# Squares of the residual stream gathered behind the eight updates and splits at seven norms of a decoder trunk

## The chip, the cores and the metric

One core of one Trainium2 chip runs the whole program. The metric is device microseconds of that core for one execution. Three runs of the kernel before gave 2433.85, 2435.99 and 2439.0 us; their median is 2435.99 us. Engines are named as in the profile: PE is TensorE (PEld its weight loads), DVE is VectorE, ACT is ScalarE, POOL is GpSimd, SP is the engine that issues the weight transfers.

## The reference, cut to what matters

The reference is a two-layer decoder trunk over 512 tokens of width 1024, in float32. Each layer adds four results to the residual stream h: a SwiGLU feed-forward (FFN, inner width 2816), a mixer, a cross-attention into 256 memory tokens, and a second FFN. Ahead of each stands an RMS norm of h, and one more stands at the very end:

```
def rmsnorm(x, g):
    y = xf * lax.rsqrt(jnp.mean(xf * xf, axis=-1, keepdims=True) + EPS)
    return y * g
...
    h = h + 0.5 * swiglu(rmsnorm(h, ffn1_norm[layer]), ...)
    hn = rmsnorm(h, mix_norm[layer])
    h = h + mix
    h = h + cross_attn(rmsnorm(h, xa_norm[layer]), mem_n, ...)
    h = h + 0.5 * swiglu(rmsnorm(h, ffn2_norm[layer]), ...)
```

The nine norms are numbered 0 to 8 in the kernel. Norm 0 works on the input, norms 1, 4 and 5 follow an FFN and lead into another projection, norms 2, 3, 6 and 7 follow an output projection (of a mixer or a cross-attention), and norm 8 is the final one.

## The kernel before, in words

**Layout.** Everything lies feature by token: h is eight chunks (k = 0 to 7) of 128 partitions by 512 tokens. A projection multiplies by weights first and is scaled by the norm's factor rstd afterwards, when its result is read from PSUM, so that PE need not wait for rstd. What PE must have is x, the gained h, split into an upper part (rounded, written by ACT in L849) and a lower part (the rest, written by DVE in L1276, `lower(k)`). Each product is three matmuls of 128x512: L310 (upper weight, upper x), L311 (upper, lower) and L312 (lower, upper).

**Weights.** A stream of 381 blocks of 128x1024 comes by DMA into two slots. POOL splits each half block in the same way: a tiny gate operation (L279), which waits until PE has left the slot, then the upper part (L280) and the lower part (L284). It takes halves in the order a, a, b, b over a pair of blocks. It takes an a half when the a half of the block two earlier has been used, and a b half when that block is done (`block_done`).

**A norm between stages.** For each chunk k, DVE waits for the finished PSUM bank and adds it to h (L1301, `h_ready`); ACT waits for that and writes the upper part of x (L849), then the square of h into one of two buffers `sq` (L871). DVE writes the lower part of chunk k-1 (L1276), then adds the square of chunk k-1 to the sum in `tg` (L1283 copies the first one, L1286 adds the other seven, `add_square`). The square k may only be written when the sum has taken in square k-2 (`sq_added`). So DVE's order is: update k, lower k-1, add k-1, update k+1, and so on.

**PE at a norm.** `project` (L340) runs the first two tiles of the next stage side by side, chunk by chunk. It waits before each chunk for the lower part of x (`x_lo`); 48 matmuls in all, six to a chunk. From chunk 4 on it also wants the b halves of both weight blocks (`split_ready`). Directly after these comes `mean_square` (L320): it waits until all eight squares are in the sum, and multiplies by a matrix of ones (L324). Only then do tiles three and four follow. ACT takes the square root (L877), DVE the reciprocal rstd (L1309), and the results of the stage are read with it (L1399, L1325).

After an FFN, PE finishes the eight PSUM banks in quick succession (six matmuls apart) and DVE follows it. After an output projection the banks come one by one, 24 matmuls apart, so that only the last chunk's update, lower part and square are left when the last tile ends.

Of the kernel before, what the change touches and what calls it, by code (L numbers as in the profile page):

```python
# [32 lines left out]
ACT = mybir.ActivationFunctionType  # L33
# [5 lines left out]
KC = D // P  # L39
# [124 lines left out]
def build_trunk(nc, xT, memT, pos, vecs, w_alpha, s5b, s5c, mats, mask, rows, stream, out):  # L164
    with ExitStack() as ctx:
        def sb(name, shape, dt=F32):
            return ctx.enter_context(nc.sbuf_tensor(name, shape, dt))
# [3 lines left out]
        def S(name):  # L171
            if name not in sems:
                sems[name] = ctx.enter_context(nc.semaphore(name))
            return sems[name]

        ps = ctx.enter_context(nc.psum_tensor("ps", [P, 8, T], F32))
        h = sb("h", [P, KC, T])
# [8 lines left out]
        sq = sb("sq", [P, 2, T])  # L186
# [37 lines left out]
        def gain(n, k):  # L224
            return vec[:, V_GAIN + 8 * n + k:V_GAIN + 8 * n + k + 1]
# [620 lines left out]
        def _(act):  # L846
            def hi(dst, src, count, **kw):

                act.activation(dst, src, ACT.Copy, **kw).then_inc(S("x_hi"), 1)  # L849

            def norm(n):

                to = NORM_TO[n] if n < 8 else None
                for k in range(KC):
                    if n == 0:
                        if k == 0:
                            act.wait_ge(S("vec_in"), 16)
                            act.wait_ge(S("x_in0"), 16)
                        if k == 2:
                            act.wait_ge(S("x_in1"), 16)  # L860
                    else:
                        act.wait_ge(S("h_ready"), 8 * (n - 1) + k + 1)
                    if to is not None:
                        if n in (1, 4, 5) and k >= 4:
                            f = {1: 0, 4: 1, 5: 2}[n]

                            act.wait_ge(S("block_done"), FFN_AT[f] + FFN_BLOCKS - (2 if k < 6 else 0))
                        hi(X[to][:, k, 0, :], h[:, k, :], 0, scale=gain(n, k))
                    if 8 * n + k >= 2:
                        act.wait_ge(S("sq_added"), 8 * n + k - 1)  # L870
                    act.activation(sq[:, k % 2, :], h[:, k, :], ACT.Square).then_inc(S("sq_ready"), 1)  # L871
                if n == 0:
                    act.wait_ge(S("eps_set"), 2)
                act.wait_ge(S("ssq_done"), n + 1)
                if n >= 1:
                    act.wait_ge(S("rstd_ready"), n)
                act.activation(std[:], ps[:, SSQ_BANK, :], ACT.Sqrt, bias=epsc[:, 0:1]  # L877
                               ).then_inc(S("std_ready"), 1)
# [336 lines left out]
            def fill(l, banks, n):  # L1215
                for _ in range(n):
                    if kv_next[0] < 16:
                        kv_out(l, kv_next[0], banks)
                        kv_next[0] += 1

            norm(0)
            ffn(0, lambda: memory_split(0), s5_begin)
            norm(1)
            s5(lambda j: fill(0, KV_BANKS, j - 13) if j >= 14 else None)
            fill(0, KV_BANKS, 2)
# [3 lines left out]
            fill(0, KV_BANKS, 16)  # L1229
            glu_split()  # L1230
            norm(2)
            cross(0)
            norm(3)
# [20 lines left out]
        def _(dve):  # L1254
# [13 lines left out]
            def norm(n, factor, mm_sem, mm_base, banks):  # L1268

                to = NORM_TO[n] if n < 8 else None  # L1270

                def lower(k):
                    if to is None:
                        return
                    dve.wait_ge(S("x_hi"), X_LO_NORM[n] + k + 1)
                    dve.scalar_tensor_tensor(X[to][:, k, 1, :], h[:, k, :], gain(n, k),  # L1276
                                             X[to][:, k, 0, :].bitcast(F32), ALU.mult, ALU.subtract
                                             ).then_inc(S("x_lo"), 1)

                def add_square(k):  # L1280
                    dve.wait_ge(S("sq_ready"), 8 * n + k + 1)
                    if k == 0:
                        ins = dve.tensor_copy(tg[:, 0, :], sq[:, 0, :])  # L1283
                    else:
                        dve.wait_ge(S("sq_added"), 8 * n + k)
                        ins = dve.tensor_tensor(tg[:, 0, :], tg[:, 0, :], sq[:, k % 2, :], ALU.add)  # L1286
                    ins.then_inc(S("sq_added"), 1)

                if n == 0:
                    for k in range(KC):  # L1290
                        lower(k)
                        add_square(k)
                else:
                    for k in range(KC):
                        if mm_sem is not None and k < 7:
                            dve.wait_ge(mm_sem, mm_base[0] + k + 1)
                        elif mm_sem is not None:
                            dve.wait_ge(S("block_done"), mm_base[1])
                        else:
                            dve.wait_ge(S("block_done"), mm_base[0] + k + 1)  # L1300
                        dve.scalar_tensor_tensor(h[:, k, :], ps[:, banks[k], :], factor, h[:, k, :],  # L1301
                                                 ALU.mult, ALU.add).then_inc(S("h_ready"), 1)
                        if k >= 1:
                            lower(k - 1)
                            add_square(k - 1)
                    lower(KC - 1)
                    add_square(KC - 1)
                dve.wait_ge(S("std_ready"), n + 1)
                dve.reciprocal(rstd[:], std[:]).then_inc(S("rstd_ready"), 1)  # L1309
                dve.wait_ge(S("rstd_ready"), n + 1)  # L1310

            def norm_after_ffn(n, f):
                norm(n, 0.5, S("down_out"), (7 * f, FFN_AT[f] + FFN_BLOCKS), DOWN_BANKS)

            def norm_after_out(n, o):
                norm(n, 1.0, None, (OUT_AT[o],), [BANKS[t % 4] for t in range(8)])
# [525 lines left out]
            dve.memset(epsc[:, 0:1], EPS).then_inc(S("eps_set"), 1)  # L1842
            dve.memset(epsc[:, 1:2], float(np.pi / 2)).then_inc(S("eps_set"), 1)
            norm(0, 1.0, None, (0,), None)
            ffn(0, lambda: memory_split(0), s5_output_matrices)
            norm_after_ffn(1, 0)
# [167 lines left out]
```

## Time and profile before

| | |
|---|---|
| median of three runs | 2435.99 us (2433.85 to 2439.0) |
| profiled execution, span from first to last instruction | 2432.6 us |
| PE busy | 2301.4 us, 95% |
| POOL busy | 1738.1 us, 71% |
| DVE busy | 1154.7 us, 47% |
| ACT busy | 435.1 us, 18% |
| mean granted TensorE clock | 0.973 |

The profiled execution has no time of its own beside its span; the three runs were executed apart from it. The median stands 3.4 us above the span. Busy time is a share of the whole span; a stretch of 20 us at a norm can be bound by another engine than the span is. In the timelines a duration is from issue to end, so that it holds the time in which an instruction stands issued and has not got what it needs.

### The profile page before, as it was taken

What the parts mean: (1) busy time and instruction counts of PE and PEld (TensorE: products, weight loads), DVE (VectorE), ACT (ScalarE), POOL (GpSimd) and SP (SyncE); (2) the same over time, 40 slices, a digit from 0 to 9 for tenths busy, and PEclk for the clock granted to TensorE, in tenths of its full rate; (3) what the DMA queues carried; (4) which work ended last, traced back from release to release, by engine and by line L of the source; (5) the groups of instructions that cost most, each with busy time, mean ns of one, the idle gap of its engine ahead of it and who ended that gap; (6) DMA issues with size and microseconds to landing.
All of it is one profiled execution on the core that took longest, in us unless ns stands there. A gap on an engine that the chain in (4) does not pass through costs nothing.

```text
span 2432.6 us, 31471 instructions
## 1 busy us (share of the span) xinstructions
PE 2301.4 (95%) x10068; PEld 1820.2 (75%) x10068; DVE 1154.7 (47%) x1468; ACT 435.1 (18%) x752; POOL 1738.1 (71%) x2287
## 2 busy tenths in 40 slices
PE   7999999888789999999999999999987999999997
PEld 6888786445678688888778888877765777888886
DVE  7577717998644342224244223144598333322314
ACT  2122212002221221111122101120134222111011
POOL 7788877565648377878787788876764746777874
PEclk9999999897889999999999999999999999999998
DMA  4244334222212123333232323332221212323332
GB/s 158 90 144 146 126 95 134 78 91 78 70 57 95 49 83 95 98 96 100 91 108 87 99 95 95 100 94 83 78 74 53 81 58 77 96 95 97 96 96 82
DMA packets 117312, 226.02 MB, mean 93 GB/s; under 512 B 13040, under 2 KB 13312, under 8 KB 116864
## 3 DMA queue, kind: packets, MB, share of 16 engines
q1 hardware_dynamic: 110736, 203.61, 26.5%
q10 hardware_dynamic: 6512, 21.52, 2.6%
q8 instruction: 45, 0.74, 0.1%
q14 instruction: 19, 0.16, 0.0%
HBM read 214.59 MB, written 10.49 MB: 93 GB/s over the span
## 4 chain that ended last, share of the span: by engine, by line
PE 79%; DVE 15%; issue 2%; ACT 2%; POOL 1%; DMA 0%; SPq 0%; ACTq 0%; DVEq 0%; POOLq 0%
PE ps L310 24%; PE ps L311 24%; PE ps L312 24%; DVE tg L1286 1%; DVE arena L1738 1%; PE ps L728 1%; DVE col L1737 1%; PE ps L753 1%; DVE x L1276 1%; DVE sg L1652 1%; PE ps L602 1%; DVE sg L1650 1%; PE ps L643 1%; PE ps L613 1%; DVE arena L1757 0%
## 5 line engine op out<-in xcount | busy, mean ns | idle before, releaser
L310 PE MATMUL ps<-x,w_split 128*128 128x512 f32 (+1 forms) x2872 | 1126.3, 392 | 39.6 <-POOL w_split L284 17.4
L311 PE MATMUL ps<-x,w_split 128*128 128x512 f32 (+1 forms) x2872 | 1110.3, 387 | 0.0
L312 PE MATMUL ps<-x,w_split 128*128 128x512 f32 (+1 forms) x2872 | 1110.0, 386 | 0.0
L284 POOL TENSOR_TENSOR w_split<-w_raw,w_split 128x512 fp32r<-128x512 f32 x762 | 1021.5, 1341 | 63.5
L279 POOL TENSOR_TENSOR gate<-gate 128x1 f32<-128x1 f32 x758 | 257.7, 340 | 602.2 <-PE ps L312 601.9
L310 PEld LDWEIGHTS ps<-x,w_split 128*128 128x128 f32 x2872 | 544.4, 190 | 180.6 <-POOL w_split L284 28.0
L311 PEld LDWEIGHTS ps<-x,w_split 128*128 128x128 f32 x2872 | 544.5, 190 | 110.1 <-issue 4.8
L312 PEld LDWEIGHTS ps<-x,w_split 128*128 128x128 f32 x2872 | 543.9, 189 | 108.8
L280 POOL TENSOR_SCALAR w_split<-w_raw 128x512 fp32r<-128x512 f32 x762 | 509.4, 669 | 4.5 <-DMA w_raw<-in_stream 4.5
L1371 DVE TENSOR_TENSOR x<-arena,x 128x512 fp32r<-128x512 f32 x88 | 87.3, 1008 | 284.6 <-ACT x L941 284.6
L1328 DVE TENSOR_TENSOR tu<-ps,rstd 128x512 f32<-128x512 f32 x88 | 60.7, 689 | 319.5 <-PE ps L312 319.5
L887 ACT ACTIVATE sg<-tg 128x512 f32<-128x512 f32 x88 | 55.6, 632 | 652.1 <-DVE tg L1325 646.9
L1325 DVE TENSOR_TENSOR tg<-ps,rstd 128x512 f32<-128x512 f32 x88 | 60.6, 689 | 192.1 <-PE ps L312 191.3
L1334 DVE TENSOR_TENSOR arena<-sg,tu 128x512 f32 (+1 forms) x88 | 107.6, 1222 | 27.3 <-ACT sg L887 17.8
L1301 DVE SCALAR_TENSOR_TENSOR h<-ps,h 128x512 f32<-128x512 f32 x64 | 44.0, 688 | 142.9 <-PE ps L312 142.4
L941 ACT ACTIVATE x<-arena 128x512 fp32r (+1 forms) x88 | 53.7, 628 | 313.1 <-PE ps L312 312.4
L849 ACT ACTIVATE x<-h,vec 128x512 fp32r<-128x512 f32 x64 | 46.2, 722 | 210.7 <-DVE h L1301 206.9
L1399 DVE TENSOR_TENSOR arena<-ps,rstd 128x512 f32<-128x512 f32 x45 | 30.7, 689 | 101.4 <-PE ps L312 100.9
L1276 DVE SCALAR_TENSOR_TENSOR x<-h,vec,x 128x512 fp32r<-128x512 f32 x64 | 67.9, 1060 | 7.9 <-ACT x L849 7.9
L1286 DVE TENSOR_TENSOR tg<-tg,sq 128x512 f32<-128x512 f32 x63 | 70.0, 1110 | 0.1
L310 PE MATMUL ps<-w_split,x 128*128 128x256 f32 (+1 forms) x192 | 66.4, 346 | 1.3 <-POOL w_split L284 1.2
L311 PE MATMUL ps<-w_split,x 128*128 128x256 f32 (+1 forms) x192 | 61.1, 318 | 0.0
(234 smaller groups left out, 1576.5 us busy)
## 6 DMA issues: line engine op xcount, KB each, us to landing
w_raw<-in_stream SPq DMA_DIRECT2D x762, 256.0 KB, 2.6
s_tables<-kv ACTq DMA_DIRECT2D x16, 512.0 KB, 3.4
arena<-s_tables ACTq DMA_DIRECT2D x16, 512.0 KB, 3.3
out<-h ACTq DMA_DIRECT2D x8, 256.0 KB, 2.2
h<-in_xT SPq DMA_DIRECT2D x1, 1536.0 KB, 8.7
arena<-in_memT SPq DMA_DIRECT2D x1, 1024.0 KB, 10.5
arena<-in_memT ACTq DMA_DIRECT2D x1, 1024.0 KB, 4.8
h<-in_xT SPq DMA_DIRECT2D x1, 512.0 KB, 3.9
```

The lines of the kernel that those rows point to most:

```text
L279: pool.tensor_tensor(gate[:, 0:1], gate[:, 1:2], gate[:, 1:2], ALU.add)
L280: pool.tensor_scalar(W[:, s, 0, c], raw[:, s, c], 1.0, 0.0, ALU.mult, ALU.add).then_inc(S(f"w_hi{'ab'[half]}"), 1)
L284: pool.tensor_tensor(W[:, s, 1, c], raw[:, s, c], W[:, s, 0, c].bitcast(F32), ALU.subtract).then_inc(split_ready if half else S("half_spli ...
L310: pe.matmul(dst, wh, xh, start=start, stop=False)
L311: pe.matmul(dst, wh, xl, start=False, stop=False)
L312: return pe.matmul(dst, wl, xh, start=False, stop=stop)
L1276: dve.scalar_tensor_tensor(X[to][:, k, 1, :], h[:, k, :], gain(n, k), X[to][:, k, 0, :].bitcast(F32), ALU.mult, ALU.subtract).then_inc(S(" ...
L1286: ins = dve.tensor_tensor(tg[:, 0, :], tg[:, 0, :], sq[:, k % 2, :], ALU.add)
L1325: dve.tensor_tensor(tg[:, s, :], ps[:, BANKS[2 * s], :], rstd[:], ALU.mult).then_inc(S("gate_ready"), 1)
L1328: dve.tensor_tensor(tu[:, s, :], ps[:, BANKS[2 * s + 1], :], rstd[:], ALU.mult).then_inc(S("up_ready"), 1)
L1334: dve.tensor_tensor(dst, sg[:, s:s + 1, :], tu[:, s:s + 1, :], ALU.mult).then_inc(S("hid_done"), 1)
L1371: dve.tensor_tensor(X[xo][:, ch:ch + 1, 1, :], hid[:, d, :], X[xo][:, ch:ch + 1, 0, :].bitcast(F32), ALU.subtract).then_inc(S("x_lo"), 1)
```

## The change

At norms 1 to 7, ACT first writes all eight upper parts and then all eight squares; DVE first does all eight updates and lower parts and then the copy and the seven additions. Norms 0 and 8 keep their order. The number of instructions, their operands and the two `sq` buffers stay as they are, and so does the order on PE, POOL and SP.

```diff
+            def square(n, k):
+                if 8 * n + k >= 2:
+                    act.wait_ge(S("sq_added"), 8 * n + k - 1)
+                act.activation(sq[:, k % 2, :], h[:, k, :], ACT.Square).then_inc(S("sq_ready"), 1)
...
                         hi(X[to][:, k, 0, :], h[:, k, :], 0, scale=gain(n, k))
-                    if 8 * n + k >= 2:
-                        act.wait_ge(S("sq_added"), 8 * n + k - 1)
-                    act.activation(sq[:, k % 2, :], h[:, k, :], ACT.Square).then_inc(S("sq_ready"), 1)
+                    if n in (0, 8):
+                        square(n, k)
+                if n not in (0, 8):
+                    for k in range(KC):
+                        square(n, k)
...
                         if k >= 1:
                             lower(k - 1)
-                            add_square(k - 1)
+                            if n == 8:
+                                add_square(k - 1)
                     lower(KC - 1)
-                    add_square(KC - 1)
+                    for k in range(KC - 1 if n == 8 else 0, KC):
+                        add_square(k)
```

## Rows read from the trace of the kernel before

**Rows 1.** The page, its first part: busy us, share, instructions of each engine

```profile
PE 2301.4 (95%) x10068; PEld 1820.2 (75%) x10068; DVE 1154.7 (47%) x1468; ACT 435.1 (18%) x752; POOL 1738.1 (71%) x2287
```

**Rows 2.** Waits of PE over the span: us in total, times, longest

```profile
PE ps L310 <- DVE x L1276: 6.9, 10, 1.3
```

**Rows 3.** Timeline of PE at norm 1: start us, us, line, [idle before <-releaser]

```profile
387.45 0.39 PE L310 MATMUL ps<-x,w_split 128*128 128x512 f32 x1
...
397.77 0.50 PE L310 MATMUL ps<-x,w_split 128*128 128x512 f32 x1 [1.31 <-DVE x L1276]
...
401.61 1.02 PE L324 MATMUL ps<-tg,ones 128*128 128x512 f32 x2
```

**Rows 4.** Timeline of DVE at norm 1: begin, a cycle, last addition

```profile
378.13 0.69 DVE L1301 SCALAR_TENSOR_TENSOR h<-ps,h 128x512 f32<-128x512 f32 x1 [1.46 <-PE ps L312]
...
380.09 1.23 DVE L1276 SCALAR_TENSOR_TENSOR x<-h,vec,x 128x512 fp32r<-128x512 f32 x1
...
388.10 0.74 DVE L1276 SCALAR_TENSOR_TENSOR x<-h,vec,x 128x512 fp32r<-128x512 f32 x1
388.76 1.77 DVE L1286 TENSOR_TENSOR tg<-tg,sq 128x512 f32<-128x512 f32 x1
390.45 0.68 DVE L1301 SCALAR_TENSOR_TENSOR h<-ps,h 128x512 f32<-128x512 f32 x1
...
399.99 0.68 DVE L1286 TENSOR_TENSOR tg<-tg,sq 128x512 f32<-128x512 f32 x1
```

**Rows 5.** Timeline of PE at norm 2: first matmul of the pair, mean square

```profile
771.71 0.39 PE L310 MATMUL ps<-x,w_split 128*128 128x512 f32 x1
...
782.59 0.59 PE L324 MATMUL ps<-tg,ones 128*128 128x512 f32 x1
```

**Rows 6.** Timeline of DVE at norm 2, last two lower parts

```profile
772.51 1.52 DVE L1276 SCALAR_TENSOR_TENSOR x<-h,vec,x 128x512 fp32r<-128x512 f32 x1
...
774.56 1.10 DVE L1276 SCALAR_TENSOR_TENSOR x<-h,vec,x 128x512 fp32r<-128x512 f32 x1
```

**Rows 7.** Timeline of POOL at norm 2

```profile
774.05 1.06 POOL L280 TENSOR_SCALAR w_split<-w_raw 128x512 fp32r<-128x512 f32 x1
775.20 1.60 POOL L284 TENSOR_TENSOR w_split<-w_raw,w_split 128x512 fp32r<-128x512 f32 x1
...
782.21 0.19 POOL L279 TENSOR_TENSOR gate<-gate 128x1 f32<-128x1 f32 x1 [0.75 <-PE ps L312]
```

**Rows 8.** Timeline of DVE, then of POOL, at norm 0

```profile
20.25 1.77 DVE L1286 TENSOR_TENSOR tg<-tg,sq 128x512 f32<-128x512 f32 x1
21.95 0.74 DVE L1276 SCALAR_TENSOR_TENSOR x<-h,vec,x 128x512 fp32r<-128x512 f32 x1
22.61 1.09 DVE L1286 TENSOR_TENSOR tg<-tg,sq 128x512 f32<-128x512 f32 x1
...
22.04 1.12 POOL L280 TENSOR_SCALAR w_split<-w_raw 128x512 fp32r<-128x512 f32 x1
```

**Rows 9.** Lines of DVE over the span: duration ns min/median/max, first, last start

```profile
L1283 DVE COPY tg<-sq x9: 412/416/839, 7.9 to 2408.6; 128x512 f32<-128x512 f32 x9
...
L1301 DVE SCALAR_TENSOR_TENSOR h<-ps,h x64: 677/692/692, 378.1 to 2416.2; 128x512 f32<-128x512 f32 x64
```

**Rows 10.** Timeline of ACT and DVE at norm 8: last square, additions six, seven

```profile
2416.91 0.63 ACT L871 ACTIVATE sq<-h 128x512 f32<-128x512 f32 x1 [0.73 <-DVE h L1301]
...
2416.79 1.48 DVE L1286 TENSOR_TENSOR tg<-tg,sq 128x512 f32<-128x512 f32 x2
```

**Rows 11.** Timeline of PE after two waits

```profile
1161.24 0.50 PE L310 MATMUL ps<-x,w_split 128*128 128x512 f32 x1 [2.45 <-DVE x L1371]
...
2418.37 2.01 PE L324 MATMUL ps<-tg,ones 128*128 128x512 f32 x2 [2.22 <-issue]
```

**Rows 12.** Two windows: us, PE, PEld, DVE, ACT, POOL busy, PEclk, DMA share, GB/s

```profile
730.00:732.00 2.00, 2.00 (x6) 1.54 (x6) 0.59 (x1) 0.00 (x0) 1.88 (x3) 0.50 0.04 8
...
2418.00:2421.00 3.00, 2.01 (x2) 0.47 (x2) 0.27 (x1) 1.42 (x2) 0.00 (x0) 0.57 0.00 0
```

## The prediction

> **What bounds the kernel now.** I read the page first, then PE's waits over the span, then the timelines of PE, DVE and POOL at the seven norms that the change touches. PE is busy for 95% of the span [rows 1], so only what starts or stops PE counts. Of its waits, ten of 6.9 us together are for the lower part of x at a norm [rows 2]; nine of them, three to a norm (0.15, 1.3 and 0.7 us), lie at norms 1, 4 and 5. At none of the seven norms does PE wait for the sum of squares.
>
> *Norms 1, 4, 5 (behind an FFN).* PE's pair of tiles starts at 387.45 and has 48 matmuls. One takes (782.59 - 771.71) / 48 = 0.2267 us undisturbed [rows 5], so the pair would end at 398.33; the mean square starts at 401.61 [rows 3]. 3.28 us are lost, for DVE is slower than PE: its cycle is update, lower part, addition, and lower part plus addition alone run from 388.10 to the next update at 390.45 [rows 4]; with the 0.60 us by which an update is issued ahead of its lower part that is 2.95 us a chunk, where six matmuls take 1.36. Norms 4 and 5 show the same to 0.02 us.
>
> *Norms 2, 3, 6, 7 (behind an output projection).* The pair starts at 771.71, and the mean square follows at 782.59 without a gap [rows 5]. The last addition ends at 777.35, 5.2 us before PE asks for the sum. So here nothing is lost. The other three repeat this to 0.1 us.
>
> **Why an addition takes 0.68 or 1.77 us.** DVE and POOL keep each other out. An addition takes 0.68 us alone the last one of [rows 4] and 1.77 us when POOL's lower part (L284) is running the one at 388.76, [rows 4]. POOL is held up in its turn: its L284 at 775.20 takes 1.60 us, behind a DVE instruction that ends at 774.56 + 1.10 = 775.66, and ends at 776.80 [rows 6, 7]. The update is never held up (677 to 692 ns in 64 cases [rows 9]); it reads PSUM and one tile of SBUF. The copy of the first square is (412 to 839 ns [rows 9]). Three numbers follow: POOL's L284 ends 1.14 us behind the DVE instruction that it waited for; its L280 ends at 775.11 [rows 7]; the DVE instruction behind POOL's ends 0.55 us later, 775.66 [rows 6].
>
> When both always have work, they take turns. At norm 0 DVE's instructions end at 22.02 (behind L284), 22.69 (free) and 23.70 (behind L280, 22.04 + 1.12 = 23.16) [rows 8]: 1.70 + 0.67 + 1.01, about 3.35 us for three DVE instructions and one split half block.
>
> The Trainium skill (SBUF — State Buffer, "Who interferes with whom") states the same as a rule: the shared port pair is an exclusive lock, and issue order decides who blocks. The trace agrees with the lock (1.77 against 0.68 us). Taken strictly, the rule says that reordering moves the blocking but doesn't remove it, which speaks against a gain.
>
> **The change, part by part.** It adds and removes no instruction. It moves eight squares on ACT and a copy and seven additions on DVE behind the eighth lower part.
>
> *Lower parts come earlier.* At norm 1 the first lower part ends at 380.09 + 1.23 = 381.3 [rows 4]. Without additions two chunks take 1.14 (POOL's L284) + 0.55 (lower part behind it) + 0.60 (update, with L280 beside it) + 0.59 (second lower part) = 2.88 us; the first such pair waits 0.4 us more, since DVE comes up to PE. The seventh lower part ends at 381.3 + 3 x 2.88 + 0.4 = 390.4, the eighth at 391.0. PE wants it at 387.45 + 7 x 1.36 = 397.0, so the 3.28 us of stall in the pair are gone, if the weights are there. PE wants the second b half before chunk 4, at 392.89; POOL ends it at 392.9, the L284 behind the copy in the next paragraph. This term is worth nothing by itself, for the mean square comes next.
>
> *The sum comes later.* ACT's squares have two buffers. Square k waits for addition k-2. At norm 8 a square starts 0.04 us behind its release, takes 0.63 us, and the last addition starts at 2416.79 + 1.48 - 0.68 = 2417.59, 0.05 us behind the square's end [rows 10]; so two additions can't be faster than 0.68 + 0.04 + 0.63 + 0.05 = 1.40, 0.70 each. The ring just keeps pace and adds 0.1 us or less to some.
>  - Norm 1: lower part ends 391.0; POOL's L280 to 391.5; copy to 391.8; POOL's L284 to 392.9; first addition 393.5; then two groups of three at 3.31 us: 396.8 and 400.1. The mean square starts at 400.1 instead of 401.61: 1.5 us gained.
>  - Norm 2: the seventh lower part ends at 774.03 [rows 6], the eighth, with no addition before it, at 774.70; L280 to 775.17; copy 775.45; L284 776.59; first addition 777.14; then 780.45 and 783.76. PE asks at 782.59 and starts at 783.8: 1.2 us lost.
>
> *What it costs PE to stand.* A matmul behind a wait takes 0.50 us instead of 0.39 [rows 3], about 0.1 us at each of seven norms: 0.7 us.
>
> *What is queued behind.* On ACT the square root stands behind the eighth square; its table load (1.28 us) fits between the last square and the mean square. On DVE the reciprocal is behind the additions, and rstd is wanted only when tiles three and four are done, 10.9 us after the mean square. It takes 0.7 + 3.4 us there. Both are hidden. On SP and POOL nothing is moved; POOL's next half waits for PE's first tile of the pair (782.21 [rows 7]) in both kernels.
>
> *Sum.* 3 x -1.5 + 4 x 1.2 + 0.7 = +1.0 us. Against the span: 2432.6 + 1.0 = 2433.6. The median stood 3.4 us above the span: **2437.0 us**.
>
> *Bounds of the unknown cost.* The trace doesn't show additions back to back with POOL at work; how often POOL gets in between is the unknown. It moves all seven norms the same way. Never: copy and seven additions take 0.35 + 7 x 0.70 = 5.25 us; the sum is ready at 396.3 and 779.95, no norm waits for it, and the whole 3 x 3.28 = 9.8 us is gained. At most: POOL has three L284 to do before it must wait for PE at norm 2; with no overlap they take 1.14 + 2 x 1.95 us (L280, L284 and gate) on top of 7 x 0.70 behind the copy's end: 775.45 + 9.9 = 785.4, 1.6 us later than my value. Seven norms so: +11.5, in all +12.5. I take the value between, as it goes by the alternation at norm 0 [rows 8], the nearest row.
>
> **Rivals.**
>  1. *One L284 less in between* (faster). If POOL's last L284 comes only behind the seventh addition, or DVE passes it over, the sum is 1.14 us earlier everywhere: norm 2 loses nothing (782.6), norm 1 gains 2.6. -7.8 + 0.7 = -7.1: 2429. With POOL left out altogether it is -9.8: 2426. For it: DVE's next instruction is issued before the last one ends. Against: at norm 0 POOL did get its turns.
>  2. *DVE pauses for each square, and POOL takes each pause* (slower). The wait for a square opens a gap of some 0.1 us behind an addition; if POOL's L280 and L284 both take one, and POOL's pieces no longer share time with DVE, the sum is up to 1.6 us later at all seven. It decides once the delay passes 0.55 us a norm (0.55 x 7 = 3.9 above +1.0). Time: some 2444, at most 2448.5.
>  3. *The clock falls while PE stands at the mean square* (slower). At norm 8 PE waited 2.22 us, and its two matmuls took 2.01 instead of 1.02 us [rows 11, 3], at a granted clock of 0.57 [rows 12], near the lower level of 1.2 GHz. The mean square would lose 1.0 us, and if the half clock of the other window [rows 12] then holds for 4 us (my assumption), 2.0 us more go with it. 3 us a norm, 21 us in all: 2458. Against it: a wait of 2.45 us left the next matmul at 0.50 us [rows 11], and the waits forecast here are 1.2 to 1.5 us.
>
> **How the numbers follow.** About 0.2% (4.9 us) is what a measurement of this kernel tells from no change. Forecast (-3 to +5 us): 0.55. Rival 1: 0.17. Rival 2: 0.23. Rival 3: 0.05. Same holds the forecast's chance, less a little that spills over: 0.54. Faster: rival 1, 0.18. Slower: rivals 2 and 3, 0.28. For 8 in 10 the range takes in most of rivals 1 and 2, from 2429.0 to 2445.0; the forecast's own range is 2433 to 2441.
>
> **What would show it.** In the profile after, PE's waits at L310 for L1276 should be gone, and a wait at L324 for the sum (`tg`, L1286) should be there seven times, at 1 to 2 us. The mean square of norm 1 should stand 22.0 us behind its first update (before: 401.61 - 378.13 = 23.5), that of norm 2 11.9 us behind the last update's start (before 10.7). Additions should be 0.68, 1.0 and 1.8 us long in turn. What would make it wrong: additions all at 0.68 (rival 1), more than four of seven held up (rival 2), or a granted clock under 1.00 at these norms (rival 3).

## The result, and the profile after

The changed kernel is **slower**: 2451.44 us (median of four runs, 2448.47 to 2453.67) against 2437.38 us for the kernel before in the same comparison. The ratio is 1.0069, with a 95% interval of 1.0046 to 1.0093, so some 17 us, 11 to 23 us; the two medians differ by 14.1 us. I had forecast 2437.0 us and a range of 2429.0 to 2445.0; the measured time lies outside it, on the side of rivals 2 and 3. The profiled execution went from a span of 2432.6 to 2451.9 us; that of the changed kernel is the longest of its four (2453.67 us), 1.8 us above its own span.

PE's waits over the span (us in total, times, longest), first in the kernel after. Before, there was no wait at the mean square (L324) at these norms, and the waits for the lower part were 6.9 us in ten pieces [rows 2].

```profile
PE ps L324 <- DVE tg L1293: 19.2, 7, 3.4
...
PE ps L310 <- DVE x L1283: 2.1, 3, 1.1
```

No wait for the lower part is left at norms 1, 4 and 5, and seven waits for the sum of squares have come. (The three that the second line counts lie at norm 0.) Here are the mean squares of norms 1 to 7, from the timeline of PE (start, us, line, and in brackets the idle time before and its releaser):

```profile
403.84 2.08 PE L324 MATMUL ps<-tg,ones 128*128 128x512 f32 x2 [3.41 <-DVE tg L1293]
787.00 1.13 PE L324 MATMUL ps<-tg,ones 128*128 128x512 f32 x2 [3.06 <-DVE tg L1293]
918.11 2.08 PE L324 MATMUL ps<-tg,ones 128*128 128x512 f32 x2 [3.06 <-DVE tg L1293]
1287.40 1.13 PE L324 MATMUL ps<-tg,ones 128*128 128x512 f32 x2 [1.75 <-DVE tg L1293]
1654.87 1.13 PE L324 MATMUL ps<-tg,ones 128*128 128x512 f32 x2 [1.75 <-DVE tg L1293]
1957.55 1.13 PE L324 MATMUL ps<-tg,ones 128*128 128x512 f32 x2 [3.06 <-DVE tg L1293]
2085.39 2.07 PE L324 MATMUL ps<-tg,ones 128*128 128x512 f32 x2 [3.06 <-DVE tg L1293]
```

All seven waits are longer than the 1.2 to 1.5 us that I had in mind. And three of the seven mean squares take 2.08 us instead of 1.02 [rows 3]. The windows (us, PE, PEld, DVE, ACT, POOL busy, PEclk, DMA share, GB/s) show why, first behind norm 1, then behind norm 2, last behind norm 4:

```profile
403.00:405.00 2.00, 1.16 (x3) 0.65 (x3) 0.79 (x1) 0.00 (x0) 1.92 (x4) 0.50 0.31 49
405.00:407.00 2.00, 2.00 (x6) 1.19 (x5) 0.33 (x1) 0.69 (x1) 0.77 (x1) 0.50 0.31 100
407.00:409.00 2.00, 2.00 (x6) 1.61 (x5) 2.00 (x1) 0.00 (x0) 0.00 (x0) 0.50 0.38 121
...
788.00:790.00 2.00, 2.00 (x7) 1.57 (x6) 1.12 (x1) 1.82 (x2) 0.94 (x1) 0.58 0.23 90
...
1287.00:1289.00 2.00, 1.60 (x5) 1.02 (x6) 0.35 (x1) 0.43 (x1) 2.00 (x3) 1.00 0.31 107
```

Behind norm 1 the granted clock is 0.50, the lower of the two levels (1.2 GHz), for the whole of these 6 us; behind norm 2 it falls only once PE works again; behind norm 4, after a wait of 1.75 us, it stays at 1.00.

DVE at norm 1 of the kernel after, as the timeline gives it (L1283 is the lower part, L1290 the copy, L1293 an addition):

```profile
379.68 0.69 DVE L1308 SCALAR_TENSOR_TENSOR h<-ps,h 128x512 f32<-128x512 f32 x1 [1.46 <-PE ps L312]
...
390.89 1.84 DVE L1283 SCALAR_TENSOR_TENSOR x<-h,vec,x 128x512 fp32r<-128x512 f32 x2
392.65 0.84 DVE L1290 COPY tg<-sq 128x512 f32<-128x512 f32 x1
393.60 10.19 DVE L1293 TENSOR_TENSOR tg<-tg,sq 128x512 f32<-128x512 f32 x7
```

ACT's fourth to sixth square in the same stretch, from the timeline of ACT:

```profile
395.22 0.63 ACT L854 ACTIVATE sq<-h 128x512 f32<-128x512 f32 x1 [1.06 <-DVE tg L1293]
396.40 0.63 ACT L854 ACTIVATE sq<-h 128x512 f32<-128x512 f32 x1 [0.54 <-DVE tg L1293]
398.10 0.63 ACT L854 ACTIVATE sq<-h 128x512 f32<-128x512 f32 x1 [1.07 <-DVE tg L1293]
```

And one turn of POOL:

```profile
395.21 0.62 POOL L280 TENSOR_SCALAR w_split<-w_raw 128x512 fp32r<-128x512 f32 x1
395.91 1.61 POOL L284 TENSOR_TENSOR w_split<-w_raw,w_split 128x512 fp32r<-128x512 f32 x1
```

The eighth lower part ends at 390.89 + 1.84 = 392.73, 13.05 us behind the first update (forecast: 12.9). The seven additions then take 10.19 us. Each square is released by an addition, so the squares' starts date the additions: they end at 395.2, 396.4, 398.1, in steps of 1.2 and 1.7 us. That is 2.9 us for **two** additions and one split half block, where I had 3.31 us for three. POOL's L280 at 395.21 takes its undisturbed 0.62 us: it got the port at the moment an addition ended, and the next addition waited for it.

### The profile page after: what moved, and what is told of

Read it like the earlier page. It is cut to its first block, busy times and chain, and to the rows that moved or that the text cites. A ratio compares the mean times of both kernels' runs of the same rounds, so it can differ in the third digit from the quotient of the medians.

```text
span 2451.9 us, 31471 instructions
## 1 busy us (share of the span) xinstructions
PE 2302.1 (94%) x10068; PEld 1817.2 (74%) x10068; DVE 1173.7 (48%) x1468; ACT 439.8 (18%) x752; POOL 1742.2 (71%) x2287
## 4 chain that ended last, share of the span: by engine, by line
PE 60%; DVE 17%; POOL 10%; issue 10%; ACT 1%; DMA 0%; POOLq 0%; SPq 0%; DVEq 0%; ACTq 0%
PE ps L310 19%; PE ps L312 18%; PE ps L311 18%; POOL w_split L284 5%; POOL w_split L280 4%; DVE tg L1293 2%; POOL gate L279 2%; DVE arena L1747 1%; DVE col L1746 1%; DVE x L1283 1%; DVE sg L1659 1%; DVE sg L1661 1%; DVE h L1308 1%; DVE tu L1668 1%; PE ps L728 1%
## 5 line engine op out<-in xcount | busy, mean ns | idle before, releaser
L310 PE MATMUL ps<-x,w_split 128*128 128x512 f32 (+1 forms) x2872 | 1127.0, 392 | 34.8 <-POOL w_split L284 19.2
L284 POOL TENSOR_TENSOR w_split<-w_raw,w_split 128x512 fp32r<-128x512 f32 x762 | 1025.7, 1346 | 63.6
L280 POOL TENSOR_SCALAR w_split<-w_raw 128x512 fp32r<-128x512 f32 x762 | 505.7, 664 | 4.6 <-DMA w_raw<-in_stream 4.6
L1293 DVE TENSOR_TENSOR tg<-tg,sq 128x512 f32<-128x512 f32 x63 | 77.9, 1236 | 5.6 <-DVE tg L1293 0.5
L1283 DVE SCALAR_TENSOR_TENSOR x<-h,vec,x 128x512 fp32r<-128x512 f32 x64 | 67.3, 1057 | 8.2 <-ACT x L849 8.0
```

The lines of the kernel that those rows point to most:

```text
L280: pool.tensor_scalar(W[:, s, 0, c], raw[:, s, c], 1.0, 0.0, ALU.mult, ALU.add).then_inc(S(f"w_hi{'ab'[half]}"), 1)
L284: pool.tensor_tensor(W[:, s, 1, c], raw[:, s, c], W[:, s, 0, c].bitcast(F32), ALU.subtract).then_inc(split_ready if half else S("half_spli ...
L310: pe.matmul(dst, wh, xh, start=start, stop=False)
```

## The experiments

My theory from the trace of the changed kernel had two parts. **Turns of two:** an addition waits for the end of the addition before it (`sq_added` at 8n + k), so DVE is never queued at the port when POOL's next instruction is, and POOL gets in between any two additions. **The clock:** PE then stands at the mean square for so long that its clock falls, which costs time beyond the wait. Rivals were the two square buffers as the cause of DVE's pauses, and a loss spread alike over all norms.

### Which norms lose

```diff
-                    if n in (0, 8):
+                    if n not in (1, 4, 5):
                         square(n, k)
-                if n not in (0, 8):
+                if n in (1, 4, 5):
...
-                            if n == 8:
+                            if n not in (1, 4, 5):
                                 add_square(k - 1)
```

> New order at norms 1, 4 and 5 alone. Theory (turns of two and the clock: POOL's split and two additions take turns, and PE stands at the mean square until the clock falls): at each of these norms the stall of 3.3 us in the pair goes, a wait at the mean square comes (3.4 us at norm 1, 1.75 us at norms 4 and 5 in the changed kernel's trace), and at norm 1 some 3 us of half clock follow. 3 x -3.3 + 6.9 + 3 + 0.3 = about +0.4 us against the kernel before, so within 3 us of it. Rival (my forecast's stepping, 1.5 us gained at each): -4.5 us.

Measured: 2436.29 us against 2436.07, ratio 0.9999 (0.9986 to 1.0013): level with the kernel before, as expected. PE's waits at its mean squares are 6.8 us in three pieces. The table under "What the norms cost, from row to row" shows that the sum behind the expectation was not right in its parts: the kernel is level without any price of the clock.

The same edit with (2, 3, 6, 7) in the place of (1, 4, 5):

> New order at norms 2, 3, 6 and 7 alone. Theory (turns of two and the clock): all the loss of the changed kernel is here, 4 x (3.1 us wait + 1 to 2 us of half clock) less what the stages behind take up: +12 to +18 us, the same as the whole change within 3 us. Rival (the loss is spread over all seven norms alike): 4/7 of it, +8 us.

Measured: 2454.59 us, ratio 1.0083 (1.0062 to 1.0103), some 20 us slower. All of the loss lies at the four norms behind an output projection, at which the kernel before lost nothing. Its waits at the mean square are 12.2 us in four pieces, so some 8 us more than the waits were lost (3 to 13, by the interval).

### What makes DVE pause

Six buffers for the squares instead of two:

```diff
+        def sq_at(n, k):
+            return sq[:, k % 2, :] if n in (0, 8) else [sq, tu, sg][k % 6 // 2][:, k % 2, :]
...
-                if 8 * n + k >= 2:
-                    act.wait_ge(S("sq_added"), 8 * n + k - 1)
-                act.activation(sq[:, k % 2, :], h[:, k, :], ACT.Square).then_inc(S("sq_ready"), 1)
+                elif k < 2 or k >= 6:
+                    act.wait_ge(S("sq_added"), 8 * n + (0 if k < 2 else k - 5))
+                act.activation(sq_at(n, k), h[:, k, :], ACT.Square).then_inc(S("sq_ready"), 1)
```

> The changed kernel with six buffers for the squares instead of two (tu and sg are free at a norm), so that ACT hardly waits for the sum. Theory A (an addition waits for the addition before it, and POOL takes the port in that pause): nothing moves, the seven additions still take 10.2 us, time within 2 us of the changed kernel. Theory B (DVE pauses because the next square is missing): additions go in turns of three, 8.3 us, the waits at the mean square are 1.9 us shorter, 10 us faster than the changed kernel.

Measured: 2454.25 us, ratio 1.0078 (1.0057 to 1.0099), the same as the change. Timeline of ACT at norm 2, the fifth and sixth square, and under it that of DVE:

```profile
776.75 1.14 ACT L860 ACTIVATE sg<-h 128x512 f32<-128x512 f32 x2
```

```profile
778.66 2.78 DVE L1299 TENSOR_TENSOR tg<-tg,tu 128x512 f32<-128x512 f32 x2
781.54 2.76 DVE L1299 TENSOR_TENSOR tg<-tg,sg 128x512 f32<-128x512 f32 x2
```

The squares in `sg` are ready at 777.9, the additions that read them begin at 781.54, and two additions still take 2.9 us. The rival falls: the squares are there, and DVE is no quicker.

Two sums, of even and odd squares, so that an addition waits only for the last but one:

```diff
+                    elif k < 2:
+                        ins = dve.tensor_copy(tg[:, k, :], sq[:, k, :])
                     else:
-                        dve.wait_ge(S("sq_added"), 8 * n + k)
-                        ins = dve.tensor_tensor(tg[:, 0, :], tg[:, 0, :], sq[:, k % 2, :], ALU.add)
+                        dve.wait_ge(S("sq_added"), 8 * n + k - 1)
+                        ins = dve.tensor_tensor(tg[:, k % 2, :], tg[:, k % 2, :], sq[:, k % 2, :], ALU.add)
...
+                        dve.tensor_tensor(tg[:, 0, :], tg[:, 0, :], tg[:, 1, :], ALU.add).then_inc(S("sum_done"), 1)
```

> The changed kernel with two sums, of even and odd squares, and one addition of the two at the end; each addition waits only for the last but one. One DVE operation more at each of the seven norms. Theory A (pause behind each addition for the one before it): DVE is queued again at once, turns of three, so copies, six additions and the last one take about 9.5 us instead of 11.1, the waits at the mean square shrink by 1.5 us each and the clock holds more often: 8 to 14 us faster than the changed kernel. Theory B (missing squares): no gain, and one more turn, 1.4 us later at each norm: 8 us or more slower.

Measured: 2452.08 us, ratio 1.0066 (1.0047 to 1.0086). Four views follow: DVE at norm 2, POOL in the same stretch, the wait of PE for the sum over the span, and two windows behind norm 3.

```profile
781.55 6.72 DVE L1302 TENSOR_TENSOR tg<-tg,sq 128x512 f32<-128x512 f32 x6
```

```profile
784.97 1.06 POOL L280 TENSOR_SCALAR w_split<-w_raw 128x512 fp32r<-128x512 f32 x1
786.12 1.60 POOL L284 TENSOR_TENSOR w_split<-w_raw,w_split 128x512 fp32r<-128x512 f32 x1
```

```profile
PE ps L327 <- DVE tg L1306: 13.1, 7, 2.3
```

```profile
917.00:919.00 2.00, 1.14 (x3) 0.64 (x3) 0.81 (x1) 0.00 (x0) 1.92 (x3) 0.81 0.45 131
919.00:921.00 2.00, 2.00 (x5) 1.34 (x4) 0.65 (x1) 1.35 (x2) 1.92 (x3) 0.50 0.36 117
```

Six additions take 6.72 us, 3.36 for three: the turns of three of my forecast (3.31), and now POOL's L280 is held up as well (1.06 us). So the wait for the addition before is what made the turns of two. The waits at the mean square went from 19.2 to 13.1 us, by 0.9 us each where 1.5 were expected. And the expected 8 to 14 us did not come: the interval overlaps that of the change. The clock did not hold more often, as I had hoped; it is at 0.50 behind norm 3 after a wait of 2.00 us. The experiment shows how DVE and POOL take turns; by its time it gains nothing that can be told from the change.

### What the clock costs

Filler matmuls ahead of PE's wait; their result is thrown away:

```diff
+                if n not in (0, 8):
+                    for _ in range(6 if n in (4, 5) else 12):
+                        pe.matmul(ps[:, SSQ_BANK, :], X[NORM_TO[n]][:, 0, 0, 0:P], X[NORM_TO[n]][:, 0, 0, :],
+                                  start=True, stop=True)
                 pe.wait_ge(S("sq_added"), 8 * n + 8)
```

> The changed kernel with filler matmuls (128x512, result thrown away) ahead of PE's wait at the mean square: 12 at norms 1, 2, 3, 6, 7 (2.7 us) and 6 at norms 4 and 5 (1.4 us). They lie in time in which PE stands anyway, so only the granted clock can change. Theory (the fallen clock is a price of its own, 1 to 3 us at each of five norms): all mean squares take 1.0 to 1.1 us, the clock stays 1.00, 7 to 10 us faster than the changed kernel, still some 9 us slower than the kernel before, for the waits themselves. Rival (the low clock is hidden by other slack): within 2 us of the changed kernel.

Measured: 2445.49 us against 2437.34, ratio 1.0040 (1.0024 to 1.0057). Timeline of PE at norm 1, where the mean square took 2.08 us without fillers, and the window just behind norm 2, where the clock of the changed kernel was 0.58 (its mean square stands at 787.00, here at 782.47):

```profile
403.80 1.13 PE L328 MATMUL ps<-tg,ones 128*128 128x512 f32 x2 [0.71 <-DVE tg L1297]
```

```profile
783.00:785.00 2.00, 2.00 (x9) 1.50 (x8) 0.64 (x1) 1.34 (x2) 1.34 (x2) 1.00 0.41 138
```

The same matmuls in the same order, with 72 more that compute nothing, and the ratio is lower than that of the change (1.0069) by 0.0029, 7 us, and than that of the run with six buffers (1.0078) by 0.0038, 9 us. These runs stand in different comparisons, each beside runs of the kernel before. Each figure is a difference of two intervals, some 7 us either way, and the first pair of intervals overlaps; the times alone make the clock's price likely and don't size it.

The traces say more. From the mean square of norm 2 to that of norm 3 it is 124.50 us before, 131.11 in the changed kernel and 127.86 with fillers. The same stretch of the other layer, from norm 6 to norm 7, takes 124.51, 127.84 and 127.84 us. So 3.3 us at each are the wait, which the fillers don't shorten, and 3.3 us more went in the first stretch of the changed kernel alone. The clock stood at 1.00 behind norm 6, and fell twice behind norm 2: directly (0.58 in the window shown above), and again at 833:

```profile
834.00:836.00 2.00, 2.00 (x7) 1.55 (x6) 0.00 (x0) 0.23 (x1) 0.00 (x0) 0.50 0.41 104
```

That is 1.6 to 1.7 us for each fall. The second doesn't belong to the wait for certain: with the old order at norm 2 (the last run of this section) the clock fell at 824 too, and the stretch took 126.20 us, 1.70 more than before. The profiled executions of the changed kernel and of this one differ by 11.6 us. Of these 4.5 lie between norms 1 and 2, 3.3 between 2 and 3, 3.2 between 3 and 4, 1.6 between 7 and 8, and none from norm 4 to norm 7, where no mean square of either has a fall behind it (the end, behind norm 8, takes 0.9 back).

What the fall behind norm 1 costs can't be read. In the stretch that follows, up to norm 2, the clock falls and rises some fifteen times in every kernel, and the stretch takes 376.7 to 383.7 us in four kernels in which nothing fell behind norm 1 and nothing was lost at norm 2. With so many other falls in it, the mean granted clock of the span (0.974 in the changed kernel, 0.973 before) doesn't show those at the norms. The scatter of the times goes with it: 23 executions of the kernel before run from 2420.83 us at a mean of 0.982 to 2440.53 us at 0.971.

Both causes taken down at once, two sums and 8 (norms 4 and 5: 6) fillers:

> The changed kernel with two sums (turns of three) and filler matmuls in PE's wait at the mean square, 8 at norms 1, 2, 3, 6, 7 (1.8 us) and 6 at norms 4 and 5. Both suspected causes are taken down at once, so what is left should be my forecast's arithmetic: waits of 13.1 us in the run with two sums, less 3 x 3.3 us of stall gained, plus 0.1 to 0.3 us for each of the seven starts behind a wait: +4 to +6 us against the kernel before. If the fallen clock did not matter: +13 us, as with two sums alone.

Measured: 2444.2 us against 2437.97, ratio 1.0038 (1.0014 to 1.0061), so 3 to 15 us slower. The expected 4 to 6 us lie in it; it shuts out neither them nor a little more.

The fillers with the new order at norms 1, 4 and 5 alone:

> New order at norms 1, 4 and 5 alone, with the same fillers there. Theory: the new order gains at these norms what its waits leave of the stall, 6.8 - 9.8 = -3 us, and only the fallen clock at norm 1 ate it (the run without fillers was level with the kernel before): 2 to 3 us faster than the kernel before. Rival (something else takes the gain back): level again, within 1 us.

Measured: medians 2432.49 against 2437.97 us, but a ratio of 0.9999 (0.9979 to 1.0020). The time doesn't decide between 3 us faster and level. The trace speaks for level: the three norms together come out 0.1 us shorter than before, not 3 (next table). So the fallen clock behind norm 1 need not have eaten anything.

### What frees the additions

The running sum in a PSUM bank that nothing else uses at that time, so that an addition reads one tile of SBUF and one of PSUM, like the update:

```diff
+                    ps0 = ps[:, SSQ_BANK, :]
                     if k == 0:
-                        ins = dve.tensor_copy(tg[:, 0, :], sq[:, 0, :])
+                        ins = dve.tensor_copy(ps0 if n else tg[:, 0, :], sq[:, 0, :])
                     else:
                         dve.wait_ge(S("sq_added"), 8 * n + k)
-                        ins = dve.tensor_tensor(tg[:, 0, :], tg[:, 0, :], sq[:, k % 2, :], ALU.add)
+                        ins = dve.tensor_tensor(tg[:, 0, :] if k == KC - 1 or n == 0 else ps0,
+                                                ps0 if n else tg[:, 0, :], sq[:, k % 2, :], ALU.add)
```

> The changed kernel with the running sum of the squares in a PSUM bank at norms 1 to 8, so that an addition reads one tile of SBUF and one of PSUM like the update, which POOL never held up. Theory (turns with POOL make the additions slow): every addition takes 0.7 us and 0.75 with the wait for the one before it, the sum is there 5.8 us after the last lower part, no wait at any mean square, no fallen clock, and the 3.3 us of stall at norms 1, 4 and 5 are gone: about 10 us faster than the kernel before. Rival (the additions are slow for their own waits, not for POOL): no gain on the changed kernel.

Measured: 2427.01 us, ratio 0.9957 (0.9944 to 0.9970), 10 us **faster** than the kernel before. The group of these additions over the span (busy us, mean ns), then the timeline of DVE at norm 1:

```profile
L1294 DVE TENSOR_TENSOR ps<-ps,sq 128x512 f32<-128x512 f32 x48 | 33.5, 699 | 4.7 <-DVE ps L1294 0.5
```

```profile
393.15 4.72 DVE L1294 TENSOR_TENSOR ps<-ps,sq 128x512 f32<-128x512 f32 x6
397.98 0.69 DVE L1294 TENSOR_TENSOR tg<-ps,sq 128x512 f32<-128x512 f32 x1
```

48 additions take 0.70 us each, whatever POOL does. One with its wait for the last takes 4.72 / 6 = 0.79 us. The wait that made the turns of two costs 0.1 us where there is no port to lose.

The same edit in the kernel before:

> The kernel before with the running sum in PSUM and its order kept. Theory (turns with POOL): DVE's cycle at norms 1, 4 and 5 shrinks from 2.95 to 2.1 to 2.4 us, for only the lower part can be held up; the lower part of chunk 7 comes at 378.1 + 8 x 2.3 = 396.5, where PE wants it at 397.0: 8 to 10 us faster than before, the same as with the new order, so that the order would be worth nothing once the additions are free. Rival (the order matters by itself): 3 us or more behind the run with both.

Measured: 2425.42 us, ratio 0.9952 (0.9937 to 0.9968). The two orders are level, and the order is worth nothing that these runs can tell. My step to it was only half right. Timeline of DVE at norm 1:

```profile
386.66 1.44 DVE L1276 SCALAR_TENSOR_TENSOR x<-h,vec,x 128x512 fp32r<-128x512 f32 x1
388.02 0.69 DVE L1287 TENSOR_TENSOR ps<-ps,sq 128x512 f32<-128x512 f32 x1
388.62 0.67 DVE L1303 SCALAR_TENSOR_TENSOR h<-ps,h 128x512 f32<-128x512 f32 x1
389.22 1.82 DVE L1276 SCALAR_TENSOR_TENSOR x<-h,vec,x 128x512 fp32r<-128x512 f32 x1
```

The addition is free, but now the lower part meets POOL each time; the cycle is 2.56 to 2.94 us, not 2.1 to 2.4. PE still waits 1.7 us at norm 1 (two waits), and none at norms 4 and 5.

Last, the sum left in SBUF, the new order at norms 1, 4 and 5, and there the mean square one tile later:

```diff
-                mean_square(n)
+                if n not in (1, 4, 5):
+                    mean_square(n)
...
                     tile(at + t, ((at + t) % 2, BANKS[t]), x)
+                    if t == 2 and n in (1, 4, 5):
+                        mean_square(n)
```

> New order at norms 1, 4 and 5 alone, and there the mean square one tile later (5.4 us), behind tile three; sum in SBUF as before. Theory: the lower parts come early enough, the sum too (it was 3.4 and 1.75 us late, now it has 5.4 us), so all of 3 x 3.3 us is gained, less about 1.5 us at norm 4, where the factor comes later to the first gate than PE wants its bank: 7 to 9 us faster than the kernel before. Rival (the late factor stops PE at the next tiles): within 3 us of it.

Measured: 2428.94 us, ratio 0.9966 (0.9955 to 0.9977), 8 us faster. So the early lower parts are worth about what the forecast said (9.8 us at most), as soon as PE has something to do while the sum is made. At norm 4 PE waits 1.0 us for its bank (expected 1.5).

### What the norms cost, from row to row

A sum of waits is not the whole loss, for PE can also come to its wait later. So here is the time from the first update of a norm (norms 1, 4, 5) or the last one (norms 2, 3, 6, 7) to the start of its mean square, as differences in us from the kernel before (23.48, 23.47, 23.48 us, and 10.68 to 10.69 us at the other four). The last column is the measured ratio times 2437 us, with its interval.

| run | norm 1 | norms 4 + 5 | norms 2 + 3 + 6 + 7 | all seven | time |
|---|---|---|---|---|---|
| forecast | -1.5 | -3.0 | +4.8 | +0.3 | +1 |
| the change | +0.7 | -0.7 | +12.9 | +12.8 | +17 (11 to 23) |
| norms 1, 4, 5 alone | +0.7 | -0.8 | 0.0 | -0.1 | 0 (-3 to +3) |
| norms 2, 3, 6, 7 alone | 0.0 | 0.0 | +12.8 | +12.9 | +20 (15 to 25) |
| six buffers | +0.7 | -0.8 | +12.8 | +12.7 | +19 (14 to 24) |
| two sums | -0.4 | -1.9 | +8.6 | +6.3 | +16 (11 to 21) |
| fillers | +0.7 | -0.8 | +13.0 | +12.9 | +10 (6 to 14) |
| two sums and fillers | -0.4 | -1.9 | +8.6 | +6.4 | +9 (3 to 15) |
| norms 1, 4, 5 with fillers | +0.7 | -0.8 | 0.0 | -0.1 | 0 (-5 to +5) |
| sum in PSUM, new order | -2.9 | -5.5 | 0.0 | -8.4 | -10 (-14 to -7) |
| sum in PSUM, old order | -1.0 | -6.6 | 0.0 | -7.5 | -12 (-15 to -8) |

The later sum costs 12.8 us at the norms themselves. The four kernels with long waits at norms 2, 3, 6 and 7 and no fillers took 4 to 10 us more than their norms account for; the three with fillers took -3 to +3 us more, and those without long waits at these norms -4 to 0. Each of these figures is uncertain by 3 to 6 us. That is the clock, in sign and rough size. At norms 4 and 5 only 0.4 us each is gained, where a stall of 3.28 went and a wait of 1.75 came. PE ends the pair 1.0 us later than forecast there. Its start is 0.3 us late; at its middle 0.4 us are lost, where POOL's b half comes late (0.27 us of it shown as a wait); the rest is the slower matmul behind each. And PE stands at the mean square some 0.16 us longer than the row's figure says.

## Why the prediction was wrong, point by point

 1. *The stall at norms 1, 4 and 5 (3.28 us each) goes.* Right. The eighth lower part came 13.05 us behind the first update, 12.9 were forecast, and PE waits for no lower part in the pair. But at norms 4 and 5 it waits 0.27 us for POOL's b half, and ends the pair 1.0 us later than forecast (0.4 at norm 1).
 2. *Three additions to one split of POOL, 3.31 us.* **Wrong; this is the step that failed.** It was taken over from norm 0 [rows 8], where additions and lower parts alternate. There each instruction is independent of the one before, and DVE is queued again at once. Seven additions in a row each wait for the last one's end. POOL, which is queued, takes the port each time: 2.87 us for two. I wrote of the wait for the squares and not of this one, though it stands in the same function. The runs with six buffers (no change) and with two sums (6.72 us for six) show which it was. At norm 2 the mean square came 787.00 - 773.09 = 13.9 us behind the start of the last update; 11.9 were forecast. At norm 1 it came 24.16 us behind the first update instead of 22.0, at norms 4 and 5 23.1. Over seven norms that is +12.8 us where the forecast had +0.3, and this one term is most of the miss.
 3. *At most 785.4 at norm 2, for POOL has only three L284 to do.* Wrong for the same reason. The additions ran on until PE's first tile of the pair was done, and a fourth L284 came in between. The last addition ended at 786.9, on a timeline that stands 1.2 us later (last update at 773.09 instead of 771.90), so at 785.7 by the old one: 0.3 us beyond what I had called the utmost. (The bound of the whole has a slip too: 11.5 and the 0.7 for standing make 12.2, not 12.5.)
 4. *Nothing lost in front of the mean square before, so four norms can only lose.* Right, and mis-sized: 1.2 us forecast; a wait of 3.06 us was measured, and a mean square 3.2 us later.
 5. *The clock (rival 3, chance 0.05).* It did fall, and the chance was too low. I priced it with waits of 1.2 to 1.5 us, but 1.5 is what norm 1 gains, not what it waits: by my own steps the wait there was 400.1 - 398.33 = 1.8 us. At 3.06 and 3.41 us the clock fell behind norms 1, 2, 3 and 7 in the profiled execution, and not behind norm 6. I had 21 us for seven norms; the traces show about 1.7 us for one fall, three of them behind norms 2, 3 and 7, and leave norm 1 open, and the times with and without fillers differ by 7 to 9 us, with a wide interval. The row that I set against it was misread. Behind the wait of 2.45 us [rows 11] the next matmul was indeed quick, but the clock fell 1 us later, in the kernel before:

```profile
1162.00:1163.00 1.00, 1.00 (x4) 0.81 (x3) 1.00 (x2) 0.00 (x0) 0.92 (x2) 0.65 0.75 229
1163.00:1165.00 2.00, 2.00 (x6) 1.52 (x5) 1.48 (x1) 0.00 (x0) 0.93 (x1) 0.50 0.03 9
```

 6. *Rival 2 (pauses let POOL in).* It held, with another pause than the one named, at all seven norms. It gives the 12.8 us of the table; the 17 us that were measured (11 to 23) leave some 4 us, in which the three falls behind norms 2, 3 and 7 find room. The two rivals were treated as exclusive, though the longer waits of the one are those behind which the clock fell.
 7. *What would show it.* The forecast named waits at L324 seven times at 1 to 2 us and additions of 0.68, 1.0 and 1.8 us in turn. The trace has seven waits, 1.75 to 3.41 us. That those of norms 4 and 5 lie in the forecast range is luck: PE and the sum are both about 1 us later than forecast.
 8. *The 3.4 us between span and median.* In every execution on record the time is 1.8 us above the span of the same execution. The other 1.6 us of my 3.4 were scatter between executions.

## What to carry to other kernels

Moving instructions past each other on an engine also changes what each stands behind: a wait on one's own last result cost nothing here while other work lay between, and gave away the place at a shared port when nothing did. Before giving PE's inputs an earlier place, look what PE asks for next, for a wait moved to the end of a stage can be longer than the ones it replaces. Size such a change from row to row, from what starts a stretch to what ends it; stalls gone and waits come don't add up to it. Look for a fallen clock some microseconds behind a wait, and not only at the first matmul. And where the sum lay in PSUM instead of SBUF, its additions took no turns with POOL at all; here that was worth 10 to 12 us in either order. (The lower parts, with both inputs in SBUF, still meet POOL.)

## What the runs showed of the hardware

An addition of 128x512 with both inputs in SBUF takes 0.68 to 1.79 us beside POOL; with one input and its output in PSUM, 0.70 us, the mean of 48. An addition that waits for the one before it took 1.44 us beside POOL with both inputs in SBUF (2.87 us for two), 1.12 us when it waited for the last but one (6.72 us for six), and 0.79 us with the sum in PSUM.

The granted clock fell to 0.50 behind waits of 3.06 to 3.41 us at four of five norms, behind one of 2.45 us in the kernel before (not behind the same wait in the kernel with fillers), and behind one of 2.00 us with two sums; behind those of 1.75 us it stayed at 1.00. It fell while PE still stood, or about 1 us after it had begun to work again, and then stayed low for 3 to 7 us. Each fall between norms 2 and 3 cost 1.6 to 1.7 us. The same wait of 3.06 us left the clock alone behind norm 6, and no run here says why.
